# TensorE takes the mixer's step of each pair ahead of that pair's value sums, in every pair of a two-branch decoder layer

## The reference

```
xn   = RMSNorm(x)
proj = xn @ w_in                       # q/k/v of attention, q/k/v/o/i/f of mLSTM, branch gates
y_sb = stick_breaking_attention(...)   # 8 heads x 64, causal
y_ml = o * headnorm(mLSTM(...))        # 4 heads x 128, chunkwise
mix  = (sigmoid(g_sb) * (y_sb @ W_sb) + sigmoid(g_ml) * (y_ml @ W_ml)) @ w_out
h    = x + mix
hn   = RMSNorm(h)
q    = hn @ w_query                    # 8 heads x 2 halves x 128
s1, s2 = q1 . keys1, q2 . keys2        # 128 keys each
top 16 of each half, top 16 of their 256 sums -> 16 experts of 16384 per head, softmax gates
act  = gelu(u[expert] . hn)            # 128 experts per token
y    = h + sum(gate * act * v[expert])
out  = RMSNorm(y)
```

## Time and profile before

| | |
|---|---|
| median of 3 runs | 3403.64 us (3398.89 to 3406.68) |
| the profiled execution | 3396.83 us, of which span 3395.0 us |
| busy: PE, PEld, DVE, ACT, POOL | 2638.8, 1343.4, 2139.4, 1080.0, 1190.3 us |
| moved by the DMA engines | 1280.41 MB, mean 377 GB/s |
| of that the gathers | 1073.81 MB, 77.0% of 16 engines' span |

### The profile page before, as it was taken

The page is one execution under the profiler, slowest core; times in us unless marked ns, Lnnn a source line. Parts: engine busy times, 40 slices in busy tenths (PEclk is TensorE's granted clock), DMA queues, the critical chain, the costliest instruction groups (busy, mean ns, idle before and its releaser), DMA issues.

```text
span 3395.0 us, 40390 instructions
## 1 busy us (share of the span) xinstructions
PE 2638.8 (78%) x14560; PEld 1343.4 (40%) x14560; DVE 2139.4 (63%) x4972; ACT 1080.0 (32%) x3398; POOL 1190.3 (35%) x1049
## 2 busy tenths in 40 slices
PE   8998887998888778988788778888787556555564
PEld 5775543565454244543344234454243111111111
DVE  2323668875457887775456797776447755775444
ACT  3111434333223553332323363332322232222222
POOL 0001332333324444343333354433334444444443
PEclk8999998999998899999898899999898776777777
DMA  3346997999999999999999989999999999999997
GB/s 113 112 130 213 411 413 280 382 412 411 417 416 418 391 376 417 419 418 416 419 413 410 374 352 398 418 418 417 414 415 418 419 399 420 421 421 410 421 421 322
DMA packets 226694, 1280.41 MB, mean 377 GB/s; under 512 B 25152, under 2 KB 27200, under 8 KB 95424
## 3 DMA queue, kind: packets, MB, share of 16 engines
q0 software_dynamic: 147456, 1073.81, 77.0%
q1 hardware_dynamic: 64128, 162.09, 13.0%
q10 hardware_dynamic: 14912, 41.95, 3.2%
HBM read 1260.97 MB, written 16.78 MB: 376 GB/s over the span
## 4 chain that ended last, share of the span: by engine, by line
DMA 38%; PE 34%; DVE 13%; ACT 6%; issue 6%; POOL 3%; ACTq 0%; POOLq 0%; DVEq 0%; SPq 0%
DMA rowsb<-uv,e_idx 37%; PE yacc L799 13%; PE mixp L514 9%; DVE rowsb L1563 6%; POOL rowsb L869 3%; PE mixp L565 3%; DVE area L1231 2%; PE mixp L526 2%; PE mixp L576 2%; ACT diag L1150 2%; ACT wg L1145 2%; PE mixp L539 1%; ACT gmt L1133 1%; DVE area L1262 1%; PE mixp L591 1%
## 5 line engine op out<-in xcount | busy, mean ns | idle before, releaser
L869 POOL DMA_INDIRECT rowsb<-uv,e_idx x1024 | 1185.6, 1158 | 2173.6 <-PE yacc L799 1688.3
L1563 DVE CUSTOM_DVE_ANT_0 rowsb<-rowsb,hnrow 128x1024 f32<-128x1024 f32 x1024 | 1242.6, 1223 | 874.7 <-DMA rowsb<-uv,e_idx 871.8
L799 PE MATMUL yacc<-rowsb,diag 64*64 64x512 f32 x8192 | 1234.9, 728 | 676.5 <-ACT diag L1150 659.7
L799 PEld LDWEIGHTS yacc<-rowsb,diag 64*64 64x64 f32 x8192 | 302.6, 152 | 1431.1 <-ACT diag L1150 990.9
L1133 ACT ACTIVATE gmt<-dots 128x2 f32<-128x2 f32 x512 | 104.1, 203 | 1800.1 <-DVE dots L1563 1799.6
L514 PE MATMUL mixp<-area,wt 128*128 128x256 f32 x2304 | 537.1, 388 | 7.2 <-ACT area L887 5.9
L514 PEld LDWEIGHTS mixp<-area,wt 128*128 128x128 f32 x2304 | 433.6, 193 | 148.3 <-issue 93.2
L1150 ACT ACTIVATE diag<-ident,wg 128x64 f32<-128x64 f32 x1024 | 300.3, 340 | 16.7
L887 ACT ACTIVATE area<-mixp 128x512 f32<-128x512 f32 (+3 forms) x384 | 163.2, 467 | 296.2 <-PE mixp L514 180.8
L1145 ACT ACTIVATE wg<-gmt,gate 128x1 f32<-128x1 f32 x1024 | 245.5, 286 | 17.5
L539 PE MATMUL mixp<-area,wt 128*128 128x256 f32 x960 | 226.6, 390 | 2.0 <-DMA wt<-w_query_ 2.0
(11 more groups left out here) (192 smaller groups left out, 1700.1 us busy)
## 6 DMA issues: line engine op xcount, KB each, us to landing
wt<-w_merge SPq DMA_DIRECT2D x96, 512.0 KB, 8.0
wt<-w_feat SPq DMA_DIRECT2D x80, 512.0 KB, 7.9
wt<-w_query_ SPq DMA_DIRECT2D x64, 512.0 KB, 12.1
wt<-w_tok SPq DMA_DIRECT2D x32, 512.0 KB, 11.4
wt<-w_out_ SPq DMA_DIRECT2D x32, 512.0 KB, 8.0
rowsb<-uv,e_idx POOLq DMA_INDIRECT x1024, 13.7
area<-x_rows ACTq DMA_DIRECT2D x4, 1024.0 KB, 12.7
area<-keysT ACTq DMA_DIRECT2D x16, 256.0 KB, 12.0
```

What stands on the lines that cost most here:

```text
L799: last = pe.matmul(yacc[at:at + HP, r, c * NCH:(c + 1) * NCH], diag[r * HP:(r + 1) * HP, s, :], rowsb[r * HP:(r + 1) * HP, s, D + c * NCH: ...
L869: pool.indirect_dma_start(rowsb[:, n % RS, :], None, uv, bass.IndirectOffsetOnAxis(ap=e_idx[:, i % 2, k:k + 1], axis=0)).then_inc(row_load ...
L1563: dve.tensor_tensor_reduce(rowsb[:, s, 0:D], rowsb[:, s, 0:D], hnrow[:, i % 2, :], 1.0, 0.0, ALU.mult, ALU.add, dots[:, s:s + 1]).then_inc ...
```

## The change: the mixer's step goes ahead of the sums in all pairs

Only PE's program is changed. The exception for pair 0 becomes the rule.

```diff
                 for i in range(TT):
                     for p in range(PP):
-                        if p > 0 or i == 0:
-                            add_rows(i, p)
                         for b in range(NB):
                             for _n in range(steps[i * PP + p][b]):
                                 next(later[b], None)
-                        if p == 0 and i > 0:
-                            add_rows(i, p)
+                        add_rows(i, p)
```

## The result

| | before | changed |
|---|---|---|
| median of 4 runs each, us | 3401.96 | 3425.95 (3422.54 to 3428.47) |
| the profiled execution, us | 3396.83 | 3426.18, of which span 3424.3 |

The ratio is 1.0074 with a 95% interval of 1.0062 to 1.0086: the change costs 21 to 29 us. That is slower by more than 0.2%, and above the predicted range (3397 to 3421). Rival (a) had 3419 to 3429. A ratio here is estimated from all executions of both kernels and need not equal the quotient of the two medians (the largest gap is 1.0058 against 1.0069, in the run with the sums of pairs 62 and 63 ahead). One execution of the experiment on bank 2 was a slow one, at 3908.16 us, and stands in no median or ratio here.

What follows compares the result with a forecast made beforehand. Bound by DMA nearly everywhere behind its start, by DVE's scans in three stretches. Terms -3 + 5 + 0 + 1 = +3 us on 3396.83 gave 3399.8; with 6.8 us to the median, 3407 predicted, range 3397 to 3421.

Steps and rivals of the forecast that it cites:

- Rival (a): Slower: the ring runs dry in MIX and attention; +15 to +25 us, so 3419 to 3429; chance 0.31.
- The third part: MIX: units of BULK wait for ACT's copy from bank 2, sums about 4.2 us late, yet taken as 0.
- the upper bound: MIX of blocks 2 and 3: eight pairs each fall short of 3.4 in flight, 1.1 us each, 18 us together.
- The mean is above 3.4, so I take 0.: Block 2's MIX: 5.2 gathers in flight, mean delay near 3 us leaves 4.2, so no loss.
- With about 3.4 in flight the DMA engines are full.: Level for judging every delay, from 640 to 780 us at DMA share 1.01; 2.7 and fewer seen not full.
- At s=0 and s=2 ... I estimate 6.5 us.: MIX steps where PE also waits for DVE and has about 2.5 us more small matmuls: sums 6.5 us late.
- Block 1's MIX: 640 to 780 us: PE busy 97%, units hardly hold anything up; taken 0, bounds -1.4 and +4 us.
- The second part: Attention of blocks 2 and 3: sums wait for same-pair ACT or DVE work; 2.5 us per block, +5 us.
- It is a lag and no rate: once PROJ2 begins the sums are on time again: Attention of blocks 2 and 3: loss per block lies between 0 and 4.3 us, the largest delay.
- The first part: End of block 1's attention: gate columns' matmul L659 starts 2.1 to 3.8 us earlier, DVE with it; -3 us.
- The fourth part: Norm of h, pair 16 of tile 1: sums 11.2 us late behind the transposes; +1 us, bounds 0 and 6.
- Its own sign: Slower rival's test: it decides once the gathers' landing time in MIX falls to about 10 us.

Runs made afterwards that it cites:

- the experiment on bank 2: The changed kernel, but in MIX ACT copies the BULK unit out of bank 2 ahead of the pair's gelu and diagonals; 3423.86 us, ratio 1.0075 to before.
- The ring of six: The kernel before with a gather ring of six places instead of eight, so every release is a pair late; 3562.52 us, ratio 1.0479.
- e2_attention: The kernel before with the step ahead of the sums only in pairs that hold a step of attention; 3411.89 us, ratio 1.0035.
- e14_values: The kernel before with the step ahead of the sums only in pairs whose attention step has value products; 3404.71 us, ratio 1.0013.

## Why the prediction was wrong

**The third part, MIX, taken at 0: wrong, and the largest part of the miss.** Alone it cost 18 us (1.0057). That this is the upper bound that I had worked out is luck: the 18 us of the bound were for blocks 2 and 3 alone, sixteen steps of 1.1 us. Of the lag that MIX ahead alone adds, 9.1 us come in block 1, where my bound was 4, and 5.7 and 4.6 in blocks 2 and 3. Three steps of the reasoning failed.

- "The mean is above 3.4, so I take 0." The mean of the delays says little. POOL's waits sum to the same (127.9 and 128.2 us); the longest went from 6.2 to 13.1, and those are the holes in the DMA row. The single delays beyond the level, which I had priced and then set aside as a bound, were the ones to count.
- "With about 3.4 in flight the DMA engines are full." The ring of six shows 0.99 at 3.4 and 0.95 at 3.2. It may be that the stretch from which I took the level, bound by PE, had a smoother release; no run tests that.
- "At s=0 and s=2 ... I estimate 6.5 us." At s=2 it was 10.2 us in the row above: PE waited 1.4 us past the diagonals for DVE's product, and the small matmuls took 4.9 us and not 2.5, at a granted clock of 0.50 behind PE's idle time (last section).

**Block 1's MIX, taken at 0:** wrong. "The same work stands between two sums in either order" holds for the work and not for the waits. PE, the bound there, had its waits covered by sums: before, L699 waited 0.2 us from 640 to 780 us. In the changed kernel:

```profile
PE mixp L699 <- DVE area L1351: 8.7, 3, 4.3
```

PE lost 6.5 us of busy time of 140, and the lag rose by 3.7 us between pair 42 of tile 0 and pair 10 of tile 1 (by 9.1 with MIX ahead alone).

**The second part, attention, +5 us:** the sign was right and the size half: +11 us alone, and the lag rose by 7.7 us in block 2 and 4.3 in block 3, PROJ2 included. "It is a lag and no rate: once PROJ2 begins the sums are on time again" held for the sums and not for the rows: behind PROJ2's first pairs DVE waits 22.6 us for them and not 12.6. It also left out that DVE, the bound there, waits for the tile's last sums (4.3 us of the lag). Which steps of attention cost the rest isn't shown: flips alone cost 20 us and value steps alone 4, but the 20 are more than all of attention cost (11).

**The first part, -3 us:** the mechanism was right and the size near, alone (5.9 to 3.4 or 1.7 us of wait, 4 to 5 us of time by the medians, with intervals that reach to 0 or just clear it). In the changed kernel 1.0 us was left of it, the wait being 4.9 us. Its PE, up to 556.26 us:

```profile
547.93 1.98 PE L637 MATMUL mixp<-area,vals_sb 128*64 128x128 f32 x16 [0.84 <-ACT area L884]
549.83 5.42 PE L799 MATMUL yacc<-rowsb,diag 64*64 64x512 f32 x32
555.18 1.08 PE L659 MATMUL mixp<-area,wif 128*68 128x256 f32 x4
```

I had let the value products of pair 28 end where they ended before, at 544.9. They end at 549.9; 3.7 us of the 5.0 is the lag at that pair. The two sums behind them take 5.4 us, near the upper end of the 3.9 to 5.6 that I had allowed. With attention's steps ahead and the gate columns too late, the wait even grew, to 7.4 and 7.5 us (e2_attention, e14_values).

**The fourth part, +1 us for the norm of h:** nothing speaks against it; the lag went from +6.9 at pair 16 of tile 1 to +7.1 at pair 24, less than one execution can tell. What I had not looked at was the norm of x. At pair 9 of tile 0 the transposes wait for DVE's scale of the same pair:

```profile
402.52 5.46 PE L591 MATMUL mixp<-area 128*128 128x128 f32 x32 [4.19 <-DVE area L1211]
...
407.92 1.95 PE L799 MATMUL yacc<-rowsb,diag 64*64 64x512 f32 x16
```

Before, these sums started at 400.39. The lag rose by 4.5 us within four pairs (10 to 14), and 1.4 us were given back by pair 16.

**PROJ1, PROJ2, out and queries at no cost:** right (1.0001).

**The rule of the Trainium skill** that the prediction weighed ("DMA: Bandwidth & Descriptors", section "Rules for kernel authors": issue a DMA early, compute, wait late) named the side on which the time came out, and the runs agree with it in that. Its reason, the fixed setup that overlaps, no run here shows; what the runs show is a ring that runs empty behind a long hold. How strictly it holds is in the measured holds, 0.2 us for one of 4.54 and 2.5 for one of 8.83: not each delay costs, but more of them than I let count.

Rival (a) had the mechanism and the time, though the time by the same luck: it priced no loss in block 1's MIX. Its own sign, a landing time near 10 us in MIX, can't be read, as the changed kernel's profile has no landing times for gathers. Open stay bank 2's own part, whether the parts overlap, and why a long hold cost less in MIX than in tiles 6 and 7.

## What to carry to other kernels

Where an engine's work gives a place in a ring back, put it ahead of that engine's other work, and let only such work pass that waits for nothing made in the same round. Judge slack by the longest single waits of the issuing queue and not by the mean number in flight: here, where some five gathers were in flight, the DMA row was flat with waits up to 8 us, dipped to 375 GB/s behind 9.5 us and had holes of 235 to 338 GB/s behind 12 to 13 us; where fewer were in flight, in the attention, 8.2 us were enough. Before moving a step, list each wait of the other engines on what it passes, at tile ends too, and look whether the bound engine is among them.

## What the runs showed of the hardware

PE's idle time ahead of a step could make the step itself longer. Behind a wait of 4.69 us the pair of matmuls L699 took 1.22 us; in block 1 of the same kernel, behind 2.40 us, it took 0.70. The granted clock (the number ahead of the DMA share) behind the first of these waits was 0.50 of full, the lower of its two levels (1.2 and 2.4 GHz), and it came back under the unit that followed:

```profile
1367.00:1370.00 3.00, 3.00 (x7) 2.04 (x8) 1.70 (x3) 0.00 (x0) 0.00 (x0) 0.50 1.04 433
1372.00:1376.00 4.00, 4.00 (x20) 3.13 (x23) 3.06 (x7) 0.15 (x1) 0.00 (x0) 0.92 1.01 418
1376.00:1382.00 6.00, 6.00 (x38) 4.12 (x30) 4.84 (x14) 3.71 (x15) 2.41 (x2) 1.00 0.80 274
```

A unit of L514 took 6.37 us behind a wait of 4.62 us (3.62 to 3.72 where PE had been busy):

```profile
1520.80 6.37 PE L514 MATMUL mixp<-area,wt 128*128 128x256 f32 x16 [4.62 <-ACT area L884]
```

The granted clock from 1330 to 1560 us fell from 0.96 to 0.90. So a wait behind which the clock falls is paid twice, once as idle time and once in the work behind it. In the run with holds of three matmuls in every pair it was the other way: PE was busy 445.40 of 500 us, the clock stood at 0.96 instead of 0.74, the sums took 1.95 us each from 3000 to 3060 us, and 128 holds of 2.84 us cost 8 us in all.
